# Rounded one-hot products and a rounded gated unit in a two-block network on Trainium2

## What is computed

```python
# the expert layer: 16 experts of 16,384 for each of 8 heads, with softmax weights
e = i1[ic // 16] * 128 + i2[ic % 16]
act = gelu(einsum('thkd,td->thk', u[e], h)) * w
y = einsum('thk,thkd->td', act, vt[e])
# the gated unit behind the state-space mixer (weights 2,048 x 2,048)
y = gelu(y)
y = y * sigmoid(y @ w_glu + b_glu)
out = (y * silu(z)) @ w_out
```

## Time and profile before

| | |
|---|---|
| median of 3 runs | 3626.04 us (3616.76 to 3626.87) |
| the profiled execution | 3616.24 us |
| its span | 3614.5 us |
| TensorE busy | 3435.4 us, 95% |
| weight loads | 3038.4 us, 84% |
| VectorE busy | 2457.7 us, 68% |
| ScalarE busy | 1337.0 us, 37% |
| GpSimd busy | 354.0 us, 10% |

### The profile page before, as it was taken

How to read it: one execution, slowest core, us unless ns; L and a number is a source line. 1 busy time by engine, 2 the same in 40 slices (tenths; PEclk the granted TensorE clock), 3 DMA queues, 4 the chain that set the end, 5 groups by cost and what they waited for, 6 DMA issues and landing times. The chain is left out here.

```text
span 3614.5 us, 56289 instructions
## 1 busy us (share of the span) xinstructions
PE 3435.4 (95%) x20628; PEld 3038.4 (84%) x20628; DVE 2457.7 (68%) x4574; ACT 1337.0 (37%) x1960; POOL 354.0 (10%) x400
## 2 busy tenths in 40 slices
PE   3899999999999999999999998999999899999998
PEld 2688887889777999999999997676679898999998
DVE  7666556867487777777777777888835634666665
ACT  1232311013244444444444444211112434555553
POOL 0010110000000000000000000677710000000000
PEclk8999999999999999999999999999999999999999
DMA  9678743446777888888888885222247644555543
GB/s 404 269 302 302 273 168 128 157 144 235 288 286 292 294 295 294 291 292 296 296 295 296 296 293 200 82 89 91 91 171 253 253 144 138 187 187 184 184 171 139
DMA packets 123316, 817.71 MB, mean 226 GB/s; under 512 B 12848, under 2 KB 18224, under 8 KB 27184
## 3 DMA queue, kind: packets, MB, share of 16 engines
q1 hardware_dynamic: 105696, 761.31, 58.4%
q10 hardware_dynamic: 17488, 54.58, 4.0%
HBM read 791.65 MB, written 24.18 MB: 226 GB/s over the span
## 5 line engine op out<-in xcount | busy, mean ns | idle before, releaser
L526 PE MATMUL bank<-H,ring 128*128 128x256 f32 x3680 | 828.8, 384 | 30.3 <-PEq L371 13.4
L526 PEld LDWEIGHTS bank<-H,ring 128*128 128x128 f32 x3680 | 696.9, 192 | 149.8 <-issue 51.3
L1833 DVE TENSOR_TENSOR vlo<-ring,vhi 128x1024 fp32r<-128x1024 f32 x448 | 547.4, 1225 | 289.1 <-ACT vhi L1241 287.8
L1241 ACT ACTIVATE vhi<-ring 128x1024 fp32r<-128x1024 f32 x448 | 474.0, 1060 | 606.9 <-PE bank L596 315.0
L562 PE MATMUL bank<-Hhi,whi 128*128 128x256 f32 x1920 | 484.9, 290 | 20.9 <-DVE Hlo L1530 9.6
L1519 DVE TENSOR_TENSOR wlo<-ring,whi 128x1024 fp32r<-128x1024 f32 x240 | 293.9, 1232 | 304.7 <-ACT whi L1054 301.4
L563 PE MATMUL bank<-Hlo,whi 128*128 128x256 f32 x1920 | 475.1, 285 | 0.0
L589 PE MATMUL bank<-vhi,Ghi 128*128 128x512 f32 x1024 | 402.0, 393 | 15.2 <-ACT vhi L1241 15.2
L590 PE MATMUL bank<-vhi,Glo 128*128 128x512 f32 x1024 | 401.1, 392 | 0.0
L562 PEld LDWEIGHTS bank<-Hhi,whi 128*128 128x128 f32 x1920 | 370.8, 193 | 31.0 <-issue 17.7
L541 PE MATMUL bank<-Fhi,vhi 128*128 128x256 f32 x1536 | 373.0, 279 | 1.1 <-ACT vhi L1241 1.1
(11 more groups left out here) (422 smaller groups left out, 4374.2 us busy)
## 6 DMA issues: line engine op xcount, KB each, us to landing
ring<-in_peer_u SPq DMA_DIRECT2D x128, 1024.0 KB, 5.7
ring<-in_peer_v SPq DMA_DIRECT2D x128, 1024.0 KB, 5.9
arena<-in_w_mod SPq DMA_DIRECT2D x96, 1024.0 KB, 7.1
ring<-in_w_ada SPq DMA_DIRECT2D x72, 1024.0 KB, 7.1
ring<-in_w_qz SPq DMA_DIRECT2D x64, 1024.0 KB, 4.8
ring<-in_w_in SPq DMA_DIRECT2D x35, 1024.0 KB, 7.3
ring<-in_ssm_in SPq DMA_DIRECT2D x32, 1024.0 KB, 5.0
ring<-in_w_mod SPq DMA_DIRECT2D x32, 1024.0 KB, 5.0
```

Of the source, the lines that this page charges most:

```text
L526: last = mm(out, ring[:, pos % R, k, :], rhs[:, k, :], start=(k == 0), stop=(k == KT - 1))
L1241: A(vhi[:, half], v_half(pos, half), ACT.Copy).then_inc(s("vhi_ready"), 1)
L1833: v.tensor_tensor(vlo[:, half], v_half(pos, half), vhi[:, half].bitcast(F32), ALU.subtract)\
```

## The change

Two stages are written anew.

- In the one-hot stage `hotA` and `hotB` become rounded tiles. VectorE first computes for all tokens the rounded weight, and the ratio of its rest to it (five operations over 256 columns). `hotB` still gets the unrounded weight, written as rounded. ScalarE makes a third tile, `hot_lo`, with three buffers: for each token `hotB` times the ratio, which is the low part, 8 activations for a unit (`lower`). The lowerings of units 0 to 2 stand ahead of the loop, that of unit k+3 behind the second copy of unit k. TensorE multiplies each token's `hotA` with `hotB` and with `hot_lo` into the same bank, one instruction each.
- The gated unit uses `gemm_split`. ScalarE rounds Y behind each piece of GELU, VectorE makes its low part, and both make the halves of the 16 weight tiles one tile ahead. The order on VectorE per output tile is: low halves of the next tile, the two products, the row's low part, and for odd tiles the reduction.

Some tiles move (`rstd1`, the buffers of the gate), and the count of halves of all later stages is shifted by 16 tiles.

```diff
-            hotA = hots.enter_context(nc.sbuf_tensor("hotA", [P, 4, 8, P], F32))
-            hotB = hots.enter_context(nc.sbuf_tensor("hotB", [P, 4, 8, P], F32))
+            hotA = hots.enter_context(nc.sbuf_tensor("hotA", [P, 4, 8, P], F32R))
+            hotB = hots.enter_context(nc.sbuf_tensor("hotB", [P, 4, 8, P], F32R))
+            hots.enter_context(nc.sbuf_tensor("hot_gap", [P, 4, T], F32))
+            hot_lo = hots.enter_context(nc.sbuf_tensor("hot_lo", [P, 3, 8, P], F32R))
...
-        LATE = dict(ssm_out=0, kv=16, nsa=40, w_o=104)
+        LATE = dict(glu=0, ssm_out=16, kv=32, nsa=56, w_o=120)
...
                 pe.wait_ge(s("hot_ready"), u + 1)
+                pe.wait_ge(s("hot_lo_ready"), u + 1)
                 for m in (2 * u, 2 * u + 1):
                     pe.wait_ge(s("spread_copied"), m + 1)
                     bank = (WA, WB, WC)[m % 3]
                     for j in range(4):
-                        last = mm(bank[:, P * j:P * j + P], hotA[:, h, 4 * (m % 2) + j, :], hotB[:, h, 4 * (m % 2) + j, :],
-                                  start=True, stop=True)
+                        t = 4 * (m % 2) + j
+                        mm(bank[:, P * j:P * j + P], hotA[:, h, t, :], hotB[:, h, t, :], start=True, stop=False)
+                        last = mm(bank[:, P * j:P * j + P], hotA[:, h, t, :], hot_lo[:, u % 3, t, :], start=False, stop=True)
                     last.then_inc(s("hot_used"), 1)
...
-            pe.wait_ge(s("y_gelu"), 4)
+            pe.sem_inc(s("half_done"), 2)
             for g in range(16):
-                gemm("glu", 0, GLU_W[g], banks[g % 4][:, 0:T], g % 4, uses[g % 4] + g // 4, Y)
+                gemm_split("glu", 0, GLU_W[g], g, banks[g % 4][:, 0:T], g % 4, uses[g % 4] + g // 4,
+                           rows=0 if g == 0 else None, pair=(Yhi, Ylo), made="y_rows")
...
+            def lower(u):
+
+                act.wait_ge(s("hot_ready"), u + 1)
+                for t in range(8):
+                    tok = 8 * u + t
+                    ins = A(hot_lo[:, u % 3, t, :], hotB[:, u % 4, t, :].bitcast(F32), ACT.Copy, scale=weight_ratio[:, tok:tok + 1])
+                ins.then_inc(s("hot_lo_ready"), 1)
+
+            for u in range(3):
+                lower(u)
...
                 for m in range(6 * c, min(6 * c + 6, 64)):
                     copy_tokens(m)
+                    if m % 2 == 1 and m // 2 + 3 < 32:
+                        lower(m // 2 + 3)
...
             for j in range(4):
-                A(Y[:, 4 * j:4 * j + 4, :], Y[:, 4 * j:4 * j + 4, :], ACT.Gelu_apprx_tanh).then_inc(s("y_gelu"), 1)
+                A(Y[:, 4 * j:4 * j + 4, :], Y[:, 4 * j:4 * j + 4, :], ACT.Gelu_apprx_tanh)
+                act.drain()
+                A(Yhi[:, 4 * j:4 * j + 4, :], Y[:, 4 * j:4 * j + 4, :], ACT.Copy).then_inc(s("yhi_ready"), 1)
+                if j == 1:
+                    high("glu", 0, GLU_W[0], 0)
             for g in range(16):
-                product(act, "glu", 0, GLU_W[g])
+                if g < 15:
+                    high("glu", 0, GLU_W[g + 1], g + 1)
+                late_product(act, "glu", g)
...
+            v.tensor_copy(weight_hi.bitcast(F32R), weight)
+            dve.drain()
+            v.tensor_tensor(weight_ratio, weight, weight_hi, ALU.subtract)
+            v.tensor_scalar(weight_inv, weight_hi, 1e-30, None, ALU.max)
+            dve.drain()
+            v.reciprocal(weight_inv, weight_inv)
+            dve.drain()
+            v.tensor_tensor(weight_ratio, weight_ratio, weight_inv, ALU.mult)
+            dve.drain()
...
+            for j in range(4):
+                dve.wait_ge(s("yhi_ready"), j + 1)
+                v.tensor_tensor(Ylo[:, 4 * j:4 * j + 4, :], Y[:, 4 * j:4 * j + 4, :],
+                                Yhi[:, 4 * j:4 * j + 4, :].bitcast(F32), ALU.subtract).then_inc(s("y_rows"), 4)
+                if j == 1:
+                    low("glu", GLU_W[0], 0)
             for g in range(16):
+                if g < 15:
+                    low("glu", GLU_W[g + 1], g + 1)
                 dve.wait_ge(s("sig_ready"), g + 1)
-                v.tensor_tensor(P2[:, g % 2, :], glt[:, g % 2, :], Y[:, g, :], ALU.mult)
+                v.tensor_tensor(gated[:, g % 2, :], glt[:, g % 2, :], Y[:, g, :], ALU.mult)
```

## The result

| | before | after |
|---|---|---|
| median | 3616.76 us, 11 runs (3613.87 to 3629.87) | 3641.28 us, 11 runs (3629.52 to 3643.56) |
| the profiled execution | 3616.24 us, span 3614.5 | 3629.52 us, span 3627.8 |
| mean granted clock in it | 0.982 | 0.977 |

The ratio of after to before is 1.005, 95% interval 1.0036 to 1.0064: slower by 0.5%, 13 to 23 us. It isn't the ratio of the medians, which lie 24.5 us apart: seven runs of before lie from 3614 to 3618 and four from 3626 to 3630, so that its median falls into the lower group; the means, 3620.0 and 3638.8, are 18.8 us apart. The profiled execution of after is the quickest of its eleven, and lies 13.3 us above that of before.

A forecast was written before the change was run, and what follows sets the result against it. TensorE's own list was taken to bound both stretches. One-hot stage +13.7 and gated unit -12.0 gave +1.7 us: 3617.9 on the profiled execution, 3628 us on the three-run median of 3626.04; range 3610 to 3650.

The forecast's parts named there:

- the first case: Whole kernel: weights' arrival paces 128-column products, ScalarE's order costs each turn 1.15 us; 3614 to 3640 us, 58%.
- rival 5: Gated unit gives nothing: paired loads land after 7 us in place of 5; total +16, 3642 us; chance 8%.
- step (c): One-hot stage: ScalarE's lowering takes 2.35 us ahead of a needed copy, 1.15 us lost per turn; +13.7 us in all.
- (a): One-hot stage, before unit 0: VectorE's added operations take 3.4 us, most of it hidden by turn 0's product.
- (b): One-hot stage, TensorE: rounded 128-column products take 0.111 to 0.120 us each; a unit stays at 1.78, at most 1.92.
- Rivals 2, 3 and 4: One-hot stage: rounded products at 0.223 us, 3671 (15%); quick product, 3620 (10%); quick product and quick lowering, 3609 (6%).
- (d): Gated unit: a product of 16 tiles takes 48 instructions of 0.120 us, 5.76 us in place of 6.89.
- (f): Gated unit: the 15 products after the first save 15 x (6.89 - 5.76), -17.0 us.
- (e): Gated unit's start: TensorE starts at 2639.75 in place of 2638.62, first product ends near 2648.5; +0.2 us.
- (g): Gated unit: VectorE keeps up, but the ring of four stalls 0.46 us six times; +2.8 us.
- (h): Passage to the next stage: later low weights end its first product at 8.5 us in place of 6.49; +2.0 us.

The follow-up runs named there:

- narrow: Changed kernel with only 64 moving columns in one-hot units 4k+1 and only 64 weight columns in units 4k+2, part of the table left out; 3645.44 us, one execution.
- late_lowering: Changed kernel with ScalarE lowering unit 3c+3 behind a turn's fourth copy and the other two behind the sixth; 3608.54 us, ratio 0.9968 to before.
- filler: Changed kernel with seven extra unused one-hot products on TensorE ahead of each wait (bank 3 and bank 6c+5); 3620.74 us, ratio 0.9989 to before.
- gated_reduction_first: Kernel before with only the gated unit's part, VectorE reducing each pair ahead of the next low halves; 3606.42 us, ratio 0.9961 to before.
- gated_only: Kernel before with only the gated unit's part of the change, one plain product per token kept; 3604.93 us, ratio 0.9958 to before.
- hots_only: Kernel before with only the one-hot part of the change, plain gemm kept for the gated unit; 3640.27 us, ratio 1.0056 to before.
- gated_again: Kernel before with only the gated unit's part of the change, measured once more; 3611.66 us, ratio 0.9969 to before.
- late_reduction_first: Changed kernel with the later lowering, and VectorE reducing each gated pair ahead of the next low halves; 3601.74 us, ratio 0.9948 to before.

## Why the prediction was wrong in its likeliest case

The time lies in the range, but not in the likeliest case: slower by 0.5%, where "no difference beyond 0.3%" had been given 60%. The forecast was +1.7 us, the means are 18.8 us apart. That 3641.28 is inside 3610 to 3650 is partly luck: the first case's own range ended at 3640, the room above it was there for rival 5, and the whole stood on a median of before of 3626.04, where eleven runs have 3616.76. None of the rivals came true either. The term that was mis-sized is that of step (c), +13.7 us for the one-hot stage, where it took +22.9. The mechanism of (c) was right; what it left out is what the idle gap does to the clock behind it.

- **(a)** right in size: VectorE's prelude took 3.4 us (776.90 to 780.31). It wasn't all hidden: ScalarE waited 0.64 us for unit 2 (790.44), and by the timeline that is most of turn 0's wait.
- **(b)** right: 0.111 us for the rounded product of 128 columns, and by narrow for the reason given as far as it was tested: the weight columns set it, not the moving ones. The 81 ns of the Trainium skill's page "TensorE: Matmul & The Clock Gate", section "Back-to-back issue gap", did not appear; 111 ns were measured. Rivals 2, 3 and 4 fall with this.
- **(c)** the lowering took 2.44 us (2.35 predicted), the sixth bank waited in each of turns 1 to 9, which cost 1.04 us (1.15), the turn was 13.30 (13.4), and the store cost 0.66 (0.6). The waits alone come to 10.9 us, less than the 13.7. The 0.83 ns of a column doesn't follow from the two rows named for it (their difference gives 0.74); the activations did follow each other 0.29 us apart, (4.79 - 2.44) / 8 by the timeline. In turn 0 the wait came two banks earlier than said, at bank 3. Missing was a term for the clock: gaps of 0.7 to 0.8 us had been priced as their own length. Behind four of the ten waits TensorE ran at 1.2 GHz, 11 to 12 us in all. late_lowering takes both away but for turn 0, filler most of the second, and their stages differ by 13.2 us (188.62 less 175.41): 9.4 of waits in nine turns, 1.5 in turn 0, and 2.3 in turns 5 and 6, for the store and the low stretch that filler keeps.
- **(d), (f)** right, a little better than said: 5.65 us for the first products (0.118 us per matmul), and 5.71 on the mean of fifteen without gaps in gated_reduction_first, where 5.76 was predicted; fifteen of them 0.8 us less than the sum had.
- **(e)** right: under 0.1 where 0.2 was said. TensorE starts 5.30 us after the GELU's start in place of 3.95, 1.3 us later where 1.1 was predicted, and that is regained in the first product.
- **(g)** right in place and cause, under-sized: six gaps, the longest idle times 0.58 and 1.08. The 89.5 us less the 85.6 without gaps leave 3.9 us for them and the one at the passage, against 2.8. gated_reduction_first removes them.
- **(h)** 1.3 us in place of 2.0: the next stage's first product took 7.77 us (2762.26 to 2770.03), 6.49 before.
- The gated part came to -12.6 us against -12.0, and by itself to ratios of 0.9958 and 0.9969. Rival 5 is refuted: some loads did land after 7 us and more (7.7 at the longest, 5.4 in the median), but the pairs cost no 2.5 us each.

Two small shares have no experiment: 1.6 us in the stretch up to the GELU and 1.4 us behind the gated unit. And why four waits of ten lost the clock stays open: 0.82 us of idle time did it twice and didn't six times.

The executions of one kernel lie up to 19 us apart, those of before too, and some 10 us of that lie outside both changed stages. The unchanged stretch from the next stage to the GELU takes 1682.5 to 1685.4 us in the traces of before, after, gated_only, gated_reduction_first and late_lowering, and 1692.8 to 1697.1 in those of hots_only, filler, gated_again and late_reduction_first. The windows view shows it in the state-space mixer, here in before and then in filler: TensorE isn't full there any more.

```profile
2480.00:2520.00 40.00, 40.00 (x170) 27.96 (x170) 33.73 (x63) 8.63 (x15) 30.52 (x36) 1.00 0.27 105
...
2480.00:2520.00 40.00, 38.20 (x162) 26.84 (x162) 34.19 (x61) 6.77 (x12) 28.09 (x32) 1.00 0.26 98
```

It may be why the median of after lies 11.8 us above its traced execution; no run shows that. What sends an execution one way or the other stays open.

## What to carry to other kernels

A short wait that an edit puts into a dense stretch of TensorE can cost twice its length, here 22 us for 11 us of waits: look behind every new gap at the granted clock, and put a price on it in the sum. When an engine with slack gets new work, its place in the queue counts, not its amount: the same 256 activations cost 22 us in front of a copy that TensorE needs and 0.9 behind it. Splitting a float32 product of 128 columns into two rounded ones gained nothing on TensorE, since the weights' columns set the pace; at 256 columns three rounded ones take 0.35 us (3 x 0.118) where the plain one takes 0.43 (6.89 / 16), and in the gated unit it paid.

## What was not expected of the hardware

- The granted clock fell to 1.2 GHz in or directly behind idle gaps of 0.68 to 1.48 us, though not at all of them, in a stretch that is otherwise full, and stayed there for several us of full work (0.74 over 790.0 to 799.4, 0.75 over 846 to 859). With other matmuls in the gap it stood at 0.99 over the stage.
- At 1.2 GHz a rounded matmul of 128 columns takes 0.21 us, twice its 0.111, although at full clock the moving columns don't set its pace. In narrow, 64 moving columns take 0.21 there as well (813.97 to 814.18), so it isn't the moving columns at the low clock either.
- Rounded matmuls of 256 columns follow each other 0.118 us apart, barely more than those of 128 with 0.111.
- Half the weight columns nearly halve the distance of rounded products of 128 moving columns, from 0.111 to 0.060 us; half the moving columns change nothing.
